# Prompt attention of a hybrid decoder step: transposed probabilities, inverse sums and the maximum

## What is computed

```python
s = einsum('btkgd,btskd->btkgs', qg, k_sel) * (HEAD_DIM ** -0.5)
dist = (q_pos[None, :, None] - sel_pos).astype(f32)
s = s - slopes[None, None, :, :, None] * dist[:, :, None, None, :]
s = where(valid[:, :, None, None, :], s, -inf)
p = softmax(s, axis=-1)
o = einsum('btkgs,btskd->btkgd', p, v_sel)
...
mix = concatenate([o_a * silu(gate_a), o_s * silu(gate_s), o_m * silu(gate_m)], axis=-1)
```

## Time and profile before

| | |
|---|---|
| median of three runs | 2048.57 us |
| profiled execution, its time | 2051.07 us |
| profiled execution, its span | 2049.5 us |
| TensorE busy in the span | 91% |
| VectorE, ScalarE, GpSimd busy | 53%, 41%, 14% |
| block "attend", from the span's start | about 1281 to 1511 us |

### The profile page before, as it was taken

The page is one execution under the profiler, slowest core; times in us unless marked ns, Lnnn a source line. Parts: engine busy times, 40 slices in busy tenths (PEclk is TensorE's granted clock), DMA queues, the critical chain, the costliest instruction groups (busy, mean ns, idle before and its releaser), DMA issues. The chain is left out here.

```text
span 2049.5 us, 31740 instructions
## 1 busy us (share of the span) xinstructions
PE 1854.8 (91%) x12954; PEld 1265.3 (62%) x12954; DVE 1093.5 (53%) x2056; ACT 839.8 (41%) x1447; POOL 293.8 (14%) x182
## 2 busy tenths in 40 slices
PE   6979999999999999999999797898887359898997
PEld 4555555556666666666666456565554148787886
DVE  5543145559876876777846026765545562122225
ACT  5454467663333433344323024543345153233431
POOL 3022211111211211112111000220022040000000
PEclk9989999999999999999999899999999569999999
DMA  8422211112222223222220631101037012222224
GB/s 328 139 73 73 67 48 57 43 63 74 91 73 85 70 75 93 70 84 74 91 73 36 240 131 61 32 21 57 1 107 248 20 63 63 64 63 64 63 74 180
DMA packets 187096, 175.93 MB, mean 86 GB/s; under 512 B 27526, under 2 KB 168486, under 8 KB 184198
## 3 DMA queue, kind: packets, MB, share of 16 engines
q1 hardware_dynamic: 166742, 133.18, 20.7%
q10 hardware_dynamic: 14640, 22.96, 3.0%
q0 software_dynamic: 5568, 17.72, 2.5%
HBM read 139.66 MB, written 34.17 MB: 85 GB/s over the span
## 5 line engine op out<-in xcount | busy, mean ns | idle before, releaser
L659 PE MATMUL ps<-h,w 128*128 128x352 f16 (+2 forms) x6096 | 947.8, 316 | 6.4 <-POOL w L932 6.1
L659 PEld LDWEIGHTS ps<-h,w 128*128 128x128 f16 (+1 forms) x6096 | 597.1, 99 | 340.1 <-issue 15.3
L2155 PE MATMUL ps<-w_f,m 128*128 128x256 f16 x3072 | 349.4, 277 | 35.1 <-POOL w_f L2094 16.7
L2155 PEld LDWEIGHTS ps<-w_f,m 128*128 128x128 f16 x3072 | 303.9, 99 | 79.0 <-POOL w_f L2094 17.8
L932 POOL TENSOR_TENSOR w<-wb,w 128x2048 f16<-128x2048 f32 (+1 forms) x45 | 186.6, 4148 | 845.3 <-ACT w L791 845.3
L799 ACT ACTIVATE zst<-ps,unit 128x352 f32<-128x352 f32 (+1 forms) x112 | 63.3, 577 | 317.2 <-PE ps L659 293.1
L1131 DVE MAX8 m<-score 128x8 f32<-128x1024 f32 (+2 forms) x192 | 171.6, 894 | 5.7
L2220 DVE SCALAR_TENSOR_TENSOR y_room<-ps,unit_f,x_f 128x256 f32 (+1 forms) x64 | 31.0, 484 | 266.4 <-PE ps L2155 242.1
L1132 DVE MATCH_REPLACE8 score<-m,score 128x1024 f32<-128x1024 f32 (+2 forms) x192 | 168.1, 876 | 0.0
L1123 DVE SCALAR_TENSOR_TENSOR score<-room,wis,score 128x1024 f32<-128x1024 f32 (+5 forms) x90 | 92.3, 1026 | 79.4 <-ACT room L854 74.3
L787 ACT ACTIVATE wb<-wb,unit 128x2048 f32<-128x2048 f32 (+1 forms) x45 | 89.5, 1988 | 90.5 <-DVE unit L946 90.5
(11 more groups left out here) (414 smaller groups left out, 1775.6 us busy)
## 6 DMA issues: line engine op xcount, KB each, us to landing
wb<-in_w_in_dram SPq DMA_DIRECT2D x44, 1024.0 KB, 5.2
z_scratch<-zst ACTq DMA_DIRECT2D x32, 528.0 KB, 2.6
score<-in_w_out_dram SPq DMA_DIRECT2D x8, 2048.0 KB, 11.6
y_room<-z_scratch SPq DMA_DIRECT2D x8, 1056.0 KB, 17.5
x_in<-in_x_prompt_dram SPq DMA_DIRECT2D x8, 1024.0 KB, 6.9
w_kv<-in_w_mem_kv_dram POOLq DMA_DIRECT2D x16, 512.0 KB, 4.9
x_f<-in_x_prompt_dram SPq DMA_DIRECT2D x8, 1024.0 KB, 5.4
out_y_p_dram<-y_room SPq DMA_DIRECT2D x8, 1024.0 KB, 3.9
```

Of the source, the lines that this page charges most:

```text
L659: last = nc.tensor.matmul(ps[0:m, n, 0:w], w16[:, b, pw_, k, 0:m], h16[:, ph, k, t0:t0 + w], start=(k == 0 and i == 0), stop=(k == KT - 1 ...
L2155: last = nc.tensor.matmul(ps[:, bank(b, t), 0:SLAB], m16[:, mp, k, t * P:(t + 1) * P], w16[:, b, wp, k, :], start=(k == 0 and j == 0), sto ...
```

## The change

Five things change together.

1. A turn becomes a plain transpose of the undivided probabilities with the identity. The diagonal matrices go, and with them ScalarE's L1626.
2. The reciprocals are made once for each unit (four columns), in the next step at head 1. SyncE writes them to DRAM, waits, and reads them back spread over all partitions; GpSimd multiplies them into `mixT` after VectorE has put in the undivided output.
3. L1669 and L1673 become one VectorE instruction that adds, scales and takes the minimum of the negated logits. ScalarE takes the exponential with scale -1.
4. For that, the projected queries leave block "project" divided by their head's slope: one more one-column operation in `set_unit` for eight chunks, and one more small ScalarE copy for each of them.
5. SyncE's loads of queries and sample keys stand between the new transfers. GpSimd's last three distance tiles are prepared between its multiplications.

```diff
@@ block_b
-        unit = sb("unit", [P, 4, 3])
+        unit = sb("unit", [P, 4, 4])
+                elif c in HEAD_OF:
+                    w_p = min(w, SEQ - t0)
+                    act.wait_ge(z_ready, before(c) + (n + 1))
+                    last = nc.scalar.activation(zst[:, sub, t0:t0 + w_p], ps[:, n, 0:w_p], ACT.Copy, scale=unit[:, c % 4, 3:4])
+                    if n == 2:
+                        last = nc.scalar.activation(zst[:, sub, SEQ:TOK], ps[:, n, w - NS:w], ACT.Copy, scale=unit[:, c % 4, 2:3])
+                    last.then_inc(z_evac, 1)
...
+                if c in HEAD_OF:
+
+                    link(TSC(unit[:, c % 4, 3:4], u[0], h_unit[:], 1.0 / SLOPES[HEAD_OF[c]], ALU.mult, ALU.mult))
@@ block_d, SyncE
-            for t in range(2, QT):
-
-                sp.wait_ge(s_mm, N_HEADS * (t - 1))
-                load_queries(sp, q_t, z_dram, t, q_loaded)
-
             sp.dma_start(v["pages"][:], io["page_table"].rearrange("b n -> (b n)").unsqueeze(0)).then_inc(v["pages_loaded"], 16)
             sp.wait_ge(v["pages_loaded"], 16)
-            sp.wait_ge(dist_ready, len(IDX_TILES))
-            for b in range(2):
-                load_keys(sp, io, v, b)
+            for u, (t, g) in enumerate(UNITS):
+                if g == 0 and 1 <= t < QT - 1:
+
+                    sp.wait_ge(s_mm, N_HEADS * t)
+                    load_queries(sp, q_t, z_dram, t + 1, q_loaded)
+                if u == len(UNITS) - 1:
+                    sp.wait_ge(dist_ready, len(IDX_TILES))
+                    for b in range(2):
+                        load_keys(sp, io, v, b)
+
+                sp.wait_ge(rinv_ready, u + 1)
+                sp.dma_start(r_dram[u], rinv[:, GQA * u:GQA * (u + 1)]).then_inc(rinv_written, 16)
+                sp.wait_ge(rinv_written, 16 * (u + 1))
+                if u >= 2:
+                    sp.wait_ge(mix_scaled, u - 1)
+                sp.dma_start(spread_inv[:, u % 2, :], r_dram[u].rearrange("p j -> (p j)").partition_broadcast(P)).then_inc(rinv_spread, 16)
@@ block_d, GpSimd
-            for t in IDX_TILES:
+            for t in IDX_TILES[:3]:
                 prepare(t)
...
+            for u, (t, g) in enumerate(UNITS):
+                if (u + 6) % 2 == 0 and (u + 6) // 2 in IDX_TILES[3:]:
+                    prepare((u + 6) // 2)
+
+                pool.wait_ge(o_used, u + 1)
+                pool.wait_ge(rinv_spread, 16 * (u + 1))
+                o = mixT[:, GQA * g:GQA * (g + 1), t * P:(t + 1) * P]
+                nc.gpsimd.tensor_tensor(o, o, spread_inv[:, u % 2, :].rearrange("p (n j) -> p j n", j=GQA), ALU.mult).then_inc(mix_scaled, 1)
@@ block_d, TensorE
-                    last = nc.tensor.matmul(ps[:, 4 + gk % 2, j * P:(j + 1) * P], pr[:, u % 2, j, k * P:(k + 1) * P],
-                                            inv_d[:, u % 2, j, :], start=True, stop=True)
+                    last = nc.tensor.transpose(ps[:, 4 + gk % 2, j * P:(j + 1) * P], pr[:, u % 2, j, k * P:(k + 1) * P], ident[:])
...
-                        pe.wait_ge(p_ready, GQA * s)
+                        pe.wait_ge(exp_done, GQA * s)
@@ block_d, ScalarE
-            def diagonal(hh):
-
-                act.wait_ge(rinv_ready, hh + 1)
-                nc.scalar.activation(inv_d[:, (hh // GQA) % 2, hh % GQA, :], ident[:], ACT.Copy, scale=rinv[:, hh:hh + 1]).then_inc(p_ready, 1)
...
-                        nc.scalar.activation(pr[:, s % 2, j, 0:n], lg[:, hh % 2, 0:n], ACT.Exp, bias=nmx[:, hh:hh + 1],
+                        nc.scalar.activation(pr[:, s % 2, j, 0:n], lg[:, hh % 2, 0:n], ACT.Exp, bias=nmx[:, hh:hh + 1], scale=-1.0,
@@ block_d, VectorE
-            def invert(hh):
-                dve.wait_ge(exp_done, hh + 1)
-                nc.vector.reciprocal(rinv[:, hh:hh + 1], rs[:, hh:hh + 1]).then_inc(rinv_ready, 1)
+            def invert(u):
+                dve.wait_ge(exp_done, GQA * (u + 1))
+                nc.vector.reciprocal(rinv[:, GQA * u:GQA * (u + 1)], rs[:, GQA * u:GQA * (u + 1)]).then_inc(rinv_ready, 1)
...
-                        nc.vector.scalar_tensor_tensor(out=lg[:, hh % 2, 0:n], in0=away,
-                                                       scalar=2.0 ** (-8.0 * (GQA * g + j + 1) / N_HEADS), in1=src,
-                                                       op0=ALU.mult, op1=ALU.add).then_inc(s_read, 1)
-                        dve.wait_ge(s_read, hh + 1)
-                        nc.vector.tensor_reduce(nmx[:, hh:hh + 1], lg[:, hh % 2, 0:n], AX_X, ALU.max, negate=True).then_inc(nm_ready, 1)
-                        if j:
-                            invert(hh - 1)
+                        nc.vector.tensor_tensor_reduce(out=lg[:, hh % 2, 0:n], in0=away, in1=src, scale=-SLOPES[GQA * g + j], scalar=3e38,
+                                                       op0=ALU.add, op1=ALU.min, accum_out=nmx[:, hh:hh + 1]).then_inc(s_read, 1)
+                    if s and j == 1:
+                        invert(s - 1)
```

More of the change, by code:

```diff
@@ L69 @@
 Z_SHIFT = 2.0 ** -12
+SLOPES = [2.0 ** (-8.0 * (h + 1) / N_HEADS) for h in range(N_HEADS)]
 def load_chunk(eng, io, wb, w_loaded, c):
@@ L124, in build_program @@
         u_dram = nc.dram_tensor("u_scratch", (D_SSM, TOK), F32, kind="Internal").ap()
+        r_dram = nc.dram_tensor("inv_scratch", (N_KV * QT, P, GQA), F32, kind="Internal").ap()
         y_dram = nc.dram_tensor("y_scratch", (D_SSM, TOK), F32, kind="Internal").ap()
@@ L476, in block_b @@
         size = sb("size", [P, 2, 4])
-        unit = sb("unit", [P, 4, 3])
+        unit = sb("unit", [P, 4, 4])
+        HEAD_OF = {c: (col - OFF_Q) // P for c, (col, _) in enumerate(CHUNKS) if OFF_Q <= col < OFF_K}
         room = sb("room", [P, 8448])
@@ L1492, in block_d @@
         prT = sb("prT", [P, 2, GQA, P])
-        inv_d = sb("inv_d", [P, 2, GQA, P])
         HEADS = QT * N_HEADS
@@ L1497, in block_d @@
         rinv = sb("rinv_d", [P, HEADS])
+        spread_inv = sb("spread_inv", [P, 2, GQA * P])
+        r_dram = v["r_dram"]
         dist_ready = sem("dist_ready")
-        s_mm, s_read, nm_ready = sem("s_mm_d"), sem("s_read_d"), sem("nm_ready_d")
-        exp_done, rinv_ready, p_ready = sem("exp_done_d"), sem("rinv_ready_d"), sem("p_ready_d")
+        s_mm, s_read = sem("s_mm_d"), sem("s_read_d")
+        exp_done, rinv_ready = sem("exp_done_d"), sem("rinv_ready_d")
+        rinv_written, rinv_spread, mix_scaled = sem("rinv_written"), sem("rinv_spread"), sem("mix_scaled")
         p_turned, p_copied = sem("p_turned_d"), [sem(f"p_copied_d{k}") for k in range(2)]
@@ L1633, in _ @@
                         hh = GQA * s + j
-                        act.wait_ge(nm_ready, hh + 1)
+                        act.wait_ge(s_read, hh + 1)
                         if j == 0 and s >= 2:
                             act.wait_ge(p_turned, first_key_block[s - 1])
-                        nc.scalar.activation(pr[:, s % 2, j, 0:n], lg[:, hh % 2, 0:n], ACT.Exp, bias=nmx[:, hh:hh + 1],
+                        nc.scalar.activation(pr[:, s % 2, j, 0:n], lg[:, hh % 2, 0:n], ACT.Exp, bias=nmx[:, hh:hh + 1], scale=-1.0,
                                              accum_out=rs[:, hh:hh + 1]).then_inc(exp_done, 1)
-                        if j:
-                            diagonal(hh - 1)
                     copy_turned(act, nc.scalar.copy, s - 1, todo[j], 0)
-                if s < len(UNITS):
-                    diagonal(GQA * s + 3)
         @block.vector
@@ L1668, in _ @@
                             dve.wait_ge(exp_done, hh - 1)
-                        nc.vector.scalar_tensor_tensor(out=lg[:, hh % 2, 0:n], in0=away,
-                                                       scalar=2.0 ** (-8.0 * (GQA * g + j + 1) / N_HEADS), in1=src,
-                                                       op0=ALU.mult, op1=ALU.add).then_inc(s_read, 1)
-                        dve.wait_ge(s_read, hh + 1)
-                        nc.vector.tensor_reduce(nmx[:, hh:hh + 1], lg[:, hh % 2, 0:n], AX_X, ALU.max, negate=True).then_inc(nm_ready, 1)
-                        if j:
-                            invert(hh - 1)
+                        nc.vector.tensor_tensor_reduce(out=lg[:, hh % 2, 0:n], in0=away, in1=src, scale=-SLOPES[GQA * g + j], scalar=3e38,
+                                                       op0=ALU.add, op1=ALU.min, accum_out=nmx[:, hh:hh + 1]).then_inc(s_read, 1)
+                    if s and j == 1:
+                        invert(s - 1)
                     copy_turned(dve, nc.vector.tensor_copy, s - 1, todo[j], 1)
-                if s < len(UNITS):
-                    invert(GQA * s + 3)
                 if s:
```

## The result

The changed kernel takes **1995.24 us**, the median of four runs (1993.13 to 1999.73); the kernel before took 2048.34 in four runs beside them (2046.55 to 2054.72). The ratio is 0.9735, with a 95% interval of 0.9715 to 0.9755: 53.1 us faster. The forecast was 2011.0, and its range began at 2003. The sign was right and the size was not.

A forecast was written before the change was run, and what follows sets the result against it. The prediction took "attend" to be bound by TensorE's work (202 of 230 us) plus 23 short waits (26 us). Its terms sum to -37.6 us, from the median 2048.57 to 2011.0 us, range 2003 to 2028.

The forecast's parts named there:

- the sentence on the barriers: Barriers stand on both sides of "attend", so what it gains moves everything behind it forward; no size of its own.
- Waits: TensorE's waits in "attend": diagonals -5.0, copies -1.4 and -7.0, new ones in steps 7 to 9 +2.0.
- The waits after the first two turns: Five waits for ScalarE's copy in "attend", 10.1 us: shorter chain but cheaper turns as cover, net -1.4.
- The turn: 72 turns in "attend", each 0.465 us as transposes in place of 0.89: -30.2 us of TensorE's work.
- The clock: Granted clock in "attend" 0.98, no term; as a rival, all work at 1.2 GHz gives 2169 us, chance 0.04.
- The fused pass: One VectorE instruction in "attend", near 1.22 us for 1024 columns plus 0.1, at some 14 remaining waits: +1.4 us.
- The rival at 2028: In "attend", the fused VectorE instruction costs as much as both old passes: 2028 us, chance 0.14.
- The hand-off's tail: At the end of "attend", only the last write, spread and GpSimd multiplication are exposed: +1.6 us.
- The queries' wait: Queries of tile 2 wait behind two SyncE writes in steps 1 to 3: +0.5 us, between 0 and 2.
- a new wait of TensorE for queries: A sign listed as showing the prediction wrong, beside a fused group above 2 us or a clock below 0.9.
- In "project": Eight chunks get one more one-column operation, 0.16 us, and one small copy: +0.5 us.
- Two-pass transposes: The transposes in "attend" keep two passes, leaving only shorter waits as gain: 2035 us, chance 0.05.

The follow-up runs named there:

- after_pad64: The changed kernel with 64 empty TensorE instructions added in block "sample": 2010.80 us, median of four, ratio 0.9806 to the kernel before.
- turns_only: The kernel before with plain transposes for the turns; diagonals still made but unused, division left out: 2029.8 us, ratio 0.9909.
- fused_only: The kernel before with the fused VectorE instruction and the queries divided by the slope, nothing else: 2026.7 us, ratio 0.9895.
- after_pad128: The changed kernel with 128 empty TensorE instructions added in block "sample": 2007.16 us in one run.

## Why the prediction was wrong in size, point by point

- **The step that failed** is the sentence on the barriers: "Barriers stand on both sides of it, so what it gains moves everything behind it forward". It left every later block unchanged. One was not: "out" lost 9.8 of the 15.5 us by which the gain of 53.1 exceeds the forecast of 37.6, 8.5 of them at two jumps of its loop, and empty instructions bring this back and take it away. Without these some 10 us the result would be about 2005, an estimate, inside the range. The nearest measurement is after_pad64, with the loop's code where it stood: 2010.80, 39.4 below the kernel before beside it (2050.24), where 37.6 was forecast. That it comes so near is partly luck, since its profile had the lower clock named above.
- **Waits.** The terms for waits and small costs in the stage, all but the tail, were -5.0 -1.4 -7.0 +2.0 +1.4 +0.5, together -9.5. All waits that the lists name went from 27.6 (26.2, the start's 1.0 and 0.4 of small ones) to 18.8: -8.8. The sum was right; within it the copies kept 15.5 of 20.0 where 13.6 was left to them, and the diagonals kept nothing where 1.2 was. The waits after the first two turns hold their place (2.19 for 2.53 at step 15), as forecast; the total hides that two parts of the change, each alone, moved them by 16 to 17 in opposite directions (turns_only 44.4, fused_only 11.2, both by all the lists' waits).
- **The turn** was mis-sized a little: 0.465 by the row of eight in the earlier trace rows, 0.44 here (0.435 is half of what the double turns take). 72 times 0.455 is 32.8, not 30.2: -2.6. (By its own numbers 0.89 - 0.465 is 0.425, which makes 30.6.)
- **The clock** was left as it was. Before, two pieces ran at 0.50 (1285.4 to 1290) and 0.62 (1406 to 1410.5); now the whole stage has 1.00. 0.02 of 230 is 4.6 us. This is not all the change's doing: the same code had 0.98 in after_pad64 and after_pad128, with 3.0 and 3.3 us more of busy time. The term was put at nothing, and of its 4.6 up to 3 may belong to the execution. The first piece in the view of stretches, in the kernel before and then in the one after:

```profile
1285.40:1290.00 4.60, 4.60 (x16) 3.56 (x16) 2.04 (x10) 2.93 (x12) 4.35 (x4) 0.50 0.08 21
```

```profile
1285.40:1290.00 4.60, 4.47 (x18) 2.91 (x18) 2.82 (x14) 2.85 (x12) 4.35 (x4) 1.00 0.32 58
```

That TensorE's other work takes 1.7 less I leave unassigned.
- **The fused pass** was right: 1.22 and 0.08 make 1.30, within "1.25 to 1.35", and the 0.1 at each wait in its term was 0.08. The rival at 2028 falls. (Its sum has 3.6 for the small terms that remain; +1.6 +0.5 +0.5 are 2.6, which makes 2027.) The Trainium skill ("DVE: opcode table, instruction layouts, handler registers and perf-mode slots", section 6, Datapath and trigger behaviour) says that a stage which reads its own previous result adds no bubble, and that the scan, which sends it back to an earlier stage, runs at half rate; the 1.22 for 1024 here and the 1.224 for 512 of the scan agree with it.
- **The hand-off's tail** was +2.8 in place of +1.6: the write behind the key loads took 3.38 to the spread's issue. The queries' wait was 1.5 in place of 0.5: "a new wait of TensorE for queries" was a sign of being wrong, and it came, though it cost 1 us more than its term. In "project" nothing was seen: "attend" began 0.1 later.
- **The rivals.** Two-pass transposes: 288 records, not 576; it falls. The clock: it went up. The Trainium skill ("TensorE: Matmul & The Clock Gate", Part 4) says that the full clock does not engage for transposes; this trace differs, with 1.00 in a stage that has 288 of them. But the rival's mechanism, long waits and then a lower clock, is there in small: the six profiles with two passes had 0.95 (turns_only) to 0.98, the eight with the fused pass 0.98 to 1.00. A single wait does not foretell it, as 1.13 and 2.08 us behind the same wait of 3.06 show.

In sum, "attend": -32.8 for turns, -4.6 clock, -1.7 unassigned, -8.8 waits, +2.8 tail, -45.1 altogether.

## What to carry to other kernels

Look at what stands ahead of a late instruction in its engine's order, not only at how long the chain is: one copy moved ahead of a wait for the logits gave 12.6 us of the block, where the whole change gave 45.1. Price a cheaper operation of the busiest engine together with the chain that its cover hid, since alone half of it turned into waits here (16.6 of 32.8 us) and 7.0 more went into longer busy time at a lower clock. Before a few us are called the change's, look at TensorE's busy time and clock in a second execution of the same code. When instructions leave an engine's stream, read also the blocks that the change does not touch, above all waits named "issue" at jumps, and run the kernel with some empty instructions before a difference of half a per cent is called the change's.

## What was not expected of the hardware

- The place of code moves waits at a loop's jump. Over all profiles of this study the same two jumps of TensorE cost 6.0 to 6.7 us in nine, 8.4 in one, and 14.5 to 15.0 in four. 64 or 192 empty instructions in the block before switch between these, and TensorE resumes 2.4 to 3.1 us after the last 16384-byte packet of queue q8 began in all of them but the one of 8.4.
- VectorE's fused add, scale and minimum over 1024 fp32 columns takes 1221 ns, no more than the plain pass, and 83 ns to hand out the result.
- TensorE's granted clock in a stage changes between executions of the same code: 1.00, 1.00, 0.98 and 0.98 in "attend" of the kernel after, with 3 us between them. Two products behind the same wait of 3.06 us took 1.13 in one run and 2.08 in another.
- GpSimd's multiplication of 512 columns with a strided operand took 1537 ns, against 1272 for its nearest contiguous row.
